# Further steps of a mixture of experts: two loops of four replaced by nested loops of two, with one step written out

## The reference, cut to what matters

```python
def _moe(h, gates, w1, w3, w2):
    y = jnp.zeros_like(h)
    for e in range(N_EXPERTS):          # 16; w1, w3: 1024 x 512, w2: 512 x 1024
        a = jax.nn.silu(h @ w1[e]) * (h @ w3[e])
        y = y + gates[..., e:e + 1].astype(h.dtype) * (a @ w2[e])
    return y
...
        w = w / jnp.sum(w, axis=-1, keepdims=True)
        x = _layernorm(DEEPNORM_ALPHA * x + g2 * yx, ln_g[l, 1], ln_b[l, 1])
```

## Time and profile before

| what | value |
|---|---|
| median of 3 runs | 1235.4 us (1234.86 to 1235.8) |
| the profiled execution's own time | 1233.08 us |
| its span | 1231.2 us |
| TensorE matmuls busy | 1009.0 us, 82% |
| VectorE, ScalarE, GpSimd busy | 335.9, 226.6, 257.7 us |
| layer 0's experts, from the first up product to the last down product | about 352 to 696 us |
| layer 1's experts | about 945 to 1195 us |
| transfers | 331.43 MB, mean 269 GB/s |

### The profile page before, as it was taken

How to read it: one execution, slowest core, us unless ns; L and a number is a source line. 1 busy time by engine, 2 the same in 40 slices (tenths; PEclk the granted TensorE clock), 3 DMA queues, 4 the chain that set the end, 5 groups by cost and what they waited for, 6 DMA issues and landing times.

```text
span 1231.2 us, 24256 instructions
## 1 busy us (share of the span) xinstructions
PE 1009.0 (82%) x9133; PEld 553.7 (45%) x9134; DVE 335.9 (27%) x787; ACT 226.6 (18%) x559; POOL 257.7 (21%) x483
## 2 busy tenths in 40 slices
PE   3899998899899888987778669998998758857860
PEld 1444756445645554543444334545445424423430
DVE  1002127523343221221111146126233312111115
ACT  0211107601321111110100123116113101000000
POOL 2000000100054333432332330000101313221431
PEclk9899999999999999998888859999998979888995
DMA  9995310290776766589899997312798999999932
GB/s 289 405 412 187 137 68 2 94 403 17 296 285 225 282 245 239 177 307 352 325 344 401 382 361 254 136 69 70 264 376 340 391 400 400 396 406 407 394 130 102
DMA packets 91142, 331.43 MB, mean 269 GB/s; under 512 B 12828, under 2 KB 15068, under 8 KB 66516
## 3 DMA queue, kind: packets, MB, share of 16 engines
q1 hardware_dynamic: 68532, 282.13, 60.3%
q0 software_dynamic: 21088, 47.48, 11.1%
q10 hardware_dynamic: 1472, 1.12, 0.3%
HBM read 303.17 MB, written 27.53 MB: 269 GB/s over the span
## 4 chain that ended last, share of the span: by engine, by line
PE 70%; DMA 11%; issue 10%; DVE 4%; SPq 2%; ACT 2%; POOL 0%; POOLq 0%; DVEq 0%; ACTq 0%
PE PS L1660 20%; PE PS L1463 17%; PE PS L1676 9%; PE PS L1580 7%; DMA W<-in_moe_w 5%; PE PS L1650 3%; DMA XT<-in_moe_w 3%; PE PS L1409 3%; PE PS L1428 2%; PE PS L1668 2%; DMA W<-in_w_in 2%; PE PS L1630 1%; SPq L575 1%; DMA H<-y_rows,DEST 1%; ACT EX L818 1%
## 5 line engine op out<-in xcount | busy, mean ns | idle before, releaser
L1660 PE MATMUL PS<-W,EX 128*32 128x256 f32 x2944 | 189.8, 414 | 57.6 <-issue 43.0
L1463 PE MATMUL PS<-W,XT 128*128 128x512 f32 (+1 forms) x544 | 216.6, 558 | 4.5 <-ACT XT L751 2.4
L1660 PEld LDWEIGHTS PS<-W,EX 128*32 128x32 f32 x2944 | 99.3, 119 | 133.5 <-issue 83.1
L1463 PEld LDWEIGHTS PS<-W,XT 128*128 128x128 f32 x544 | 103.2, 191 | 112.1 <-issue 107.2
L721 ACT ACTIVATE AT<-EX 64x512 f32<-64x512 f32 x64 | 40.4, 631 | 420.8 <-PE PS L1650 393.2
L617 POOL TENSOR_TENSOR RSTD<-VAR,HALF 128x1 f32<-128x1 f32 (+1 forms) x24 | 16.3, 683 | 476.8 <-DVE VAR L997 476.8
L1289 DVE COPY EX<-PS 128x256 f32<-128x256 f32 x66 | 28.0, 424 | 314.5 <-PE PS L1660 314.4
L1660 PE MATMUL PS<-RAB,EX 128*32 128x256 f32 x640 | 84.2, 421 | 35.0 <-DMA XT<-in_moe_w 19.8
L648 POOL DMA_DIRECT2D y_rows<-AT x136 | 67.5, 497 | 185.7 <-DVE AT L1299 175.8
L648 POOL DMA_DIRECT2D y_rows<-EX x128 | 63.5, 496 | 157.6 <-DVE EX L1299 142.3
L1676 PE MATMUL PS<-W,AT 128*32 128x256 f32 x1472 | 90.9, 388 | 1.5 <-DVE AT L1296 1.5
(11 more groups left out here) (192 smaller groups left out, 1001.4 us busy)
## 6 DMA issues: line engine op xcount, KB each, us to landing
W<-in_moe_w SPq DMA_DIRECT2D x66, 2048.0 KB, 18.5
W<-in_w_ada SPq DMA_DIRECT2D x24, 2048.0 KB, 14.5
RAB<-in_moe_w SPq DMA_DIRECT2D x10, 2048.0 KB, 20.2
XT<-in_moe_w SPq DMA_DIRECT2D x10, 2048.0 KB
H<-in_moe_w SPq DMA_DIRECT2D x10, 2048.0 KB, 13.3
W<-in_w_in SPq DMA_DIRECT2D x8, 2048.0 KB, 25.8
EX<-xg_rows POOLq DMA_DIRECT2D x136, 64.0 KB, 5.8
W<-in_w_out SPq DMA_DIRECT2D x4, 2048.0 KB, 12.3
```

What stands on the lines that cost most here:

```text
L1463: mm = pe.matmul(ps[:, 0:cw], XT[:, k, P * t:P * t + P], w[:, k, :], start=(k == 0), stop=(k == KD - 1))
L1660: mm = pe.matmul(UP_PS[o:o + ROWS, 0:256], rows, moe_up(p, n)[:, k, 256 * a:256 * a + 256], start=(k == 0), stop=(k == KD - 1), tile_posit ...
```

## The change

The nest of two loops of further steps is replaced, on TensorE alone. `again(j)` is one further step. `further(first, n)` runs steps `first` to `first + n - 1` by halves: a loop of two rounds, each with a branch around the same again for half as many, down to a single step. For p = 0 all further steps go through it (16 in layer 0, 8 in layer 1). For p = 1 and 2, two of the three experts of a round, the second step is written by itself in front, and only a third or later one goes into the loops.

```diff
-                    with pe.If(cnt > ROWS):
-                        with pe.Fori(0, T) as g:
-                            with pe.If(cnt > g * (4 * ROWS) + ROWS):
-                                with pe.Fori(0, 4) as i:
-                                    with pe.If(cnt > g * (4 * ROWS) + i * ROWS + ROWS):
-                                        j = 4 * g + i
-                                        pe.wait_ge(xgt_ready[L], step + j + 2)
-                                        up(p)
-                                        rest(p, step + j + 1, p, own)
-                                    with pe.Else():
-                                        pe.nop()
+                    def again(j):
+
+                        pe.wait_ge(xgt_ready[L], step + j + 1)
+                        up(p)
+                        rest(p, step + j, p, own)
+
+                    def further(first, n):
+
+                        if n == 1:
+                            again(first)
+                            return
+                        with pe.Fori(0, 2) as half:
+                            begin = first + half * (n // 2)
+                            with pe.If(cnt > begin * ROWS):
+                                further(begin, n // 2)
                             with pe.Else():
                                 pe.nop()
+
+                    with pe.If(cnt > ROWS):
+                        if p:
+                            again(1)
+                            with pe.If(cnt > 2 * ROWS):
+                                further(2, 4 * T)
+                                pe.nop()
+                        else:
+                            further(1, 4 * T)
                         pe.nop()
```

## The result

The kernel after the change takes 1305.0 us (median of 4 runs, 1300.8 to 1308.4) against 1235.4 for the kernel before: 1.055 times as long, 95% interval 1.052 to 1.0585. The forecast was 1222 with a range of 1216 to 1234, so the change makes the kernel some 70 us slower where 13.7 us of gain were forecast.

The account below looks back on a forecast made before the run. Layer 0 was taken as bound by TensorE with little room under it, layer 1 by weights until all are in. Gains of 9.8 + 3.9 = 13.7 us, code at nothing, took 1235.4 to 1222 us, range 1216 to 1234.

Parts of the forecast that it names:

- the term for code: TensorE's instruction queue over the experts' rounds: a round grows to nine blocks with the one fetched ahead; cost taken as nothing.
- The price: TensorE's stop for an instruction block that isn't there: 2.77 us, read off one wait at 960.4; used only in the rivals.
- Rival (b): Experts' rounds: each pushed-out block pushes out the next, some three misses or 8.4 us a round; 1247 us, chance 0.18.
- Rival (a): One block fetched anew at each jump back, 2.8 us, four times a layer; 1230 us, chance 0.15.
- eight are held now: Argument against nine blocks causing fetches: the old rounds' eight blocks are kept without a fetch.
- The gaps: TensorE idle between experts: none behind two-step experts with p not 0, 3.4 us behind 6 and 9, 2.6 behind 4.
- 9.8 + 3.9 us: Gains: layer 0's expert 15 starts 9.8 us earlier, limited by weights; layer 1's tail from expert 12 gains 3.9.
- the forecast rate: Weight transfers in layer 0's experts: 390 to 400 GB/s from 555 us on, where 336 ran during two-step experts.
- 2.4: Layer 0's experts 0 to 5 together end 2.4 us later, from the nested loops and entering two levels more.
- The sum behind them: Whole kernel: 9.8 us from layer 0 and 3.9 from layer 1 add to 13.7 us gained.
- their loads are queued behind the experts' and come earlier too: Between layer 0's experts and layer 1's: that stretch's loads come earlier too, so all moves by the 9.8 us.

Follow-up runs that it names:

- 3: Kernel before the change plus 228 TensorE instructions that never run in each expert of p = 2: 1238.3 us, ratio 1.001.
- 4: Kernel before the change plus 264 TensorE instructions that never run in each expert of p = 2: 1296.0 us, ratio 1.047.
- 5: The changed kernel with the second step written in front for p = 2 alone: 1271.8 us, 1.0305 of the kernel before.
- 6: Same code as 5, but with the head of each layer's loop of rounds at a block's start: 1229.1 us, 0.996 of the kernel before.
- 7: The whole changed kernel with a hint on the loop of rounds that it will jump back: 1229.2 us, 0.996 of the kernel before.
- 8: Kernel before with its two loops of four replaced by one loop whose bounds are the steps in registers: 1199.3 us, ratio 0.973.
- 11: The kernel of 8, unchanged, run again beside two other kernels on one chip: 1199.0 us.
- 10: The kernel of 8 with only half the rows of some of layer 1's w_ada loads: 1194.3 us, 0.965 of the kernel before.

## Why the prediction was wrong

**The step that failed** is the term for code: "Whether nine stay is not shown; I take nothing, and keep the price for the rivals." The count, nine, was right, and in layer 0 so was the place, the jump back. Nine do not stay: 3 and 4, 5 and 6, and the change itself and 7 each cross the threshold in their own way, and each time the kernel loses at nine and not at eight (1296.0 and 1238.3 us, 1271.8 and 1229.1, 1305.0 and 1229.2). So a term put at nothing was 70 us. What is held is eight blocks of 16,384 bytes, as the runs show it: 34 to 39 fetches at seven or eight, 72 to 89 at nine. The count that decides includes the block fetched ahead: without it the whole change has 38 fetches (7), with it 89.

**The price** failed with it. 2.77 us came from one wait in the earlier trace rows, and there the block's packets begin 0.2 us after TensorE stops (960.59 and 960.38). Where they begin later the stop is longer: 2.9 us after it in experiment 7, a stop of 5.36 us, and 2.1 to 3.0 us after it at the jumps back of after, stops of 7.1 to 8.0 us, with a slower clock behind them (1.5 to 1.7 us in the 32 matmuls). Rival (b) had the mechanism, each block pushing out the next, and its sign; it gave 1247, since it took three misses of 2.8 us a round and a layer 1 mostly covered by its weights. Layer 1 in fact fetched 45 blocks, stood 30.2 us longer with no wait for weights left, and lost 10.8 to the clock. Rival (a) describes the number of blocks in the first rounds of layer 0 (two for each jump back) but at nearly three times its price. A chance of 0.18 for all of that was too low, given that the prediction had the count in hand and put "eight are held now" against it, which says nothing of nine.

**The gaps** were right where they can be read. Behind two-step experts with p not 0 none is left (596.48 in the chain). Behind expert 6 it is 3.56 us (3.4 forecast), behind 5 3.5 and 9 3.68, behind 4 2.65 (2.6), and behind 3 1.90 (1.8). Entering two levels more shows no idle time in the chain.

**9.8 + 3.9 us** seem to stand in 6, where the code stays: 10.0 and 4.3 in the experts of the two layers, and a wait for the weights of 9.4 us that takes the place of the gaps, as argued. But 6 isn't the whole change: the gaps of p = 1 are still there. The whole change with its code kept is 7, and there it is 5.3 and 3.2, with the 5.36 us at the exit still to come. The transfers do run at the forecast rate in 7 (376, 389 and 402 GB/s in the three stretches of 20 us from 580 us on). What differs is the delay ahead of them. Counted from the first up product, expert 6 starts 4.7 us later than before in 6 and 8.6 in 7, where 2.4 were forecast, so the loads behind it are asked for later; expert 15 starts 8.7 us earlier in 6 and 3.9 in 7, where 9.8 were forecast. Whether the 2.4 was wrong or these executions were late the runs don't show: in 3, where nothing that runs is changed but a jump, expert 6 starts 4.5 us later too. So 9.8 is met by 6 alone, which lacks half of the front steps, and that is in part luck.

**The sum behind them** was too good. The step "their loads are queued behind the experts' and come earlier too" failed: they don't come earlier by as much, and 4 to 7 us of the experts' gain are given back there in 6, 8 and 11, and not in the run with half loads (10). So without the ninth block the change brought 6 us (7, with the stop at the exit in it), and not 13.7.

**Open.** Why a jump back costs 7 to 8 us when the block's packets take about one: in after they lie in 582.8 to 583.9 us, the matmuls ended at 579.79 and go on at 587.80. At all four jumps back of layer 0 it takes 3.9 to 4.1 us from the landing of the block to the next product, and only 1.4 to 1.5 in 7's exit and at the wait of the earlier trace rows. Why three rounds of layer 0 in after bring two blocks each and the last one nearly all, while 4 and 5 bring 18 and 21 blocks between 485 and 650 us already.

## What to carry to other kernels

Count the instructions of a loop's body on the engine before adding a copy of anything in it, in blocks (some 253 recorded instructions each) and with the block behind its end: here nine in place of eight turned a gain of 0.4% into a loss of 5.5%, and 36 instructions that never run cost 4.7%. Where it is near the edge, the place of the loop's head (1271.8 to 1229.1 us) or a hint for its jump back (1305.0 to 1229.2) decides; better is code that is shorter, as a loop with its own bounds: it gave the front step's gain and more (0.973 of the time before) with fewer blocks. When a stage bound by transfers becomes faster, look at the loads queued behind it: here they were the next wait (3.6 us before, 13.7 in 6).

## What the runs showed of the hardware that was not expected

- In these kernels TensorE's sequencer keeps eight blocks of 16 KB over a loop's rounds. A ninth brings 72 to 89 fetched blocks in place of 35 to 39 at eight, in two patterns: only the blocks around the jump (two for each, layer 0's first rounds of after) or nearly every block (45 in the 282 us of its layer 1).
- Stops of this kind also fall into the middle of a product, and the granted clock is lower with them: 0.84 over layer 1's experts against 0.89.
- A hint for the jump back keeps the block behind the loop from being fetched, and moves its cost to the exit: 5.36 us in layer 0, none that the trace shows in layer 1.
- Loops whose bounds come from registers show no idle at their turns in layer 0: no wait of "issue" stands ahead of its up products in 8 (39.1 us before), and those ahead of L1650 stay as they were (16 of at most 1.7 us, against 15 of at most 1.8).
